# Hybrid decoder layer on one core: gating stage run as two passes over the tokens

## What is computed

```python
gate = jax.nn.sigmoid(_rmsnorm(h, g_ple) @ w_ple_gate)   # w_ple_gate 1024 x 1024
h = h + gate * (p @ w_ple)                               # w_ple 256 x 1024
...
y_prompt = _rmsnorm(hp, g_final)
y_sample = _rmsnorm(hs, g_final)
```

## Time and profile before

| what | value |
|---|---|
| median of 3 runs | 918.92 us (918.61 to 921.02) |
| profiled execution, its time | 919.41 us |
| its span | 917.6 us |
| granted TensorE clock, mean of full | 0.996 |
| TensorE busy | 904.3 us, 99% of the span |
| VectorE, ScalarE, GpSimd busy | 535.4, 370.0, 237.9 us |

### The profile page before, as it was taken

How to read it: one execution, slowest core, us unless ns; L and a number is a source line. 1 busy time by engine, 2 the same in 40 slices (tenths; PEclk the granted TensorE clock), 3 DMA queues, 4 the chain that set the end, 5 groups by cost and what they waited for, 6 DMA issues and landing times.

```text
span 917.6 us, 21039 instructions
## 1 busy us (share of the span) xinstructions
PE 904.3 (99%) x8016; PEld 894.6 (97%) x8016; DVE 535.4 (58%) x651; ACT 370.0 (40%) x511; POOL 237.9 (26%) x289
## 2 busy tenths in 40 slices
PE   9999999999999999999999999999999999999995
PEld 8999999999999999999999999999999999999995
DVE  6432279888765565665576666666666433435654
ACT  7323446556554555233343333333333222213433
POOL 0006078777111100004621111111111122213441
PEclk9999999999999999999999999999999999999998
DMA  7322534233245443533323333333333333332312
GB/s 227 104 87 88 184 94 105 59 98 97 72 129 157 114 131 108 192 119 100 92 70 95 90 91 91 91 91 91 91 91 109 96 94 94 94 92 66 107 36 94
DMA packets 176479, 94.84 MB, mean 103 GB/s; under 512 B 17888, under 2 KB 174960, under 8 KB 176016
## 3 DMA queue, kind: packets, MB, share of 16 engines
q1 hardware_dynamic: 149698, 80.61, 29.6%
q10 hardware_dynamic: 26736, 13.60, 5.5%
HBM read 86.25 MB, written 8.03 MB: 103 GB/s over the span
## 4 chain that ended last, share of the span: by engine, by line
PE 75%; DVE 5%; issue 3%; ACT 1%; ACTq 0%; DVEq 0%
PE acc L502 69%; DVE rs L1409 1%; DVE sfull L1396 1%; PE lvb L502 1%; DVE xs L1400 0%; PE mb L764 0%; PE lvb L728 0%; PE ob L743 0%; PE mb L747 0%; PE ob L742 0%; DVE ss L1449 0%; PE lvb L644 0%; DVE ot L1411 0%; DVE ss L1447 0%; PE lvb L852 0%
## 5 line engine op out<-in xcount | busy, mean ns | idle before, releaser
L908 ACT ACTIVATE whi<-raw 128x1024 fp32r<-128x1024 f32 (+2 forms) x132 | 146.8, 1112 | 369.6 <-PE acc L502 368.7
L1277 DVE TENSOR_TENSOR wlo<-raw,whi 128x1024 fp32r<-128x1024 f32 (+2 forms) x131 | 196.5, 1500 | 151.8 <-ACT whi L908 151.8
L502 PE MATMUL acc<-xah,whi 128*128 128x260 f32 x896 | 184.7, 287 | 0.0
L502 PE MATMUL acc<-xah,wlo 128*128 128x260 f32 x896 | 180.3, 283 | 0.0
L502 PE MATMUL acc<-xal,whi 128*128 128x260 f32 x896 | 179.9, 282 | 0.0
L502 PE MATMUL acc<-xbh,whi 128*128 128x260 f32 x816 | 165.0, 283 | 0.0
L502 PE MATMUL acc<-xbh,wlo 128*128 128x260 f32 x816 | 164.4, 283 | 0.0
L502 PE MATMUL acc<-xbl,whi 128*128 128x260 f32 x816 | 164.2, 283 | 0.0
L502 PEld LDWEIGHTS acc<-xah,whi 128*128 128x128 f32 x896 | 137.9, 188 | 1.5 <-issue 0.2
L502 PEld LDWEIGHTS acc<-xal,whi 128*128 128x128 f32 x896 | 138.0, 188 | 0.0
L502 PEld LDWEIGHTS acc<-xah,wlo 128*128 128x128 f32 x896 | 137.9, 188 | 0.0
(11 more groups left out here) (310 smaller groups left out, 1175.6 us busy)
## 6 DMA issues: line engine op xcount, KB each, us to landing
raw<-in_w_in SPq DMA_DIRECT2D x96, 256.0 KB, 3.1
raw<-in_w_up SPq DMA_DIRECT2D x88, 256.0 KB, 3.1
raw<-in_w_down SPq DMA_DIRECT2D x16, 384.0 KB, 3.5
raw<-in_w_down SPq DMA_DIRECT2D x16, 320.0 KB, 3.9
raw<-in_w_out SPq DMA_DIRECT2D x16, 256.0 KB, 3.1
raw<-in_w_ple_gate SPq DMA_DIRECT2D x8, 512.0 KB, 3.8
x_transposed<-xstg SPq DMA_DIRECT2D x1, 2080.0 KB, 7.6
hT<-x_transposed ACTq DMA_DIRECT2D x1, 2080.0 KB, 8.0
```

The lines of the kernel that those rows point to most:

```text
L502: mm = pe.matmul(sums[:, b, 0:HT], wt[slot][:, w], xx[:, c, b * HT:(b + 1) * HT], start=first and i == 0 and q == 0, stop=last and i == n ...
L908: act.activation(whi[k % 2][:, 0:n], raw[k % 2][:, 0:n], ACT.Copy).then_inc(hi_ready, 1)
L1277: dve.tensor_tensor(wlo[k % 2][:, 0:n], raw[k % 2][:, 0:n], whi[k % 2][:, 0:n].bitcast(fp), SUB).then_inc(lo_ready, 1)
```

## The change

The 520 tokens are taken in two passes (HSPLIT: 256 tokens, then 264). Step n of 16 makes channel tile n % 8 for the tokens of its pass: 24 gate and 6 embedding matmuls of 256 or 264 columns. The weights are loaded and copied to `whi` in both passes; the low parts of tiles 2 to 7 are kept in six new buffers `wlh`, and those of tiles 0 and 1 in `wlo`, so that VectorE subtracts in the first pass only. `tg`, `sgg`, `tp` and the PSUM sums are doubled. The addition to `hT` moves from VectorE to GpSimd for all steps but the last. PE's first two steps are interleaved (`first_steps`). The y transposes go by pairs of tiles and one pass's tokens (`y_pair`), the first behind step 3. The scale of the first 256 tokens is taken behind step 10, applied in step 12, and their two output DMAs are issued from there. VectorE's order at the end of G changes: the `xbl` of the last tile now comes ahead of the low part of unit H1.

```diff
-YSPLIT = 384
+YSPLIT = 448
+HSPLIT = (256, TT - 256)
...
-            for it in range(2):
-                for k in range(4):
-                    load("H", k, it, [wpg_v[:, :, it * 4 + k, :], wpl_v[:, :, it * 4 + k, :]])
-                if it == 0:
+            for n in range(2 * DC):
+                load("H", n, 0, [wpg_v[:, :, n % DC, :], wpl_v[:, :, n % DC, :]], low=n < DC + 2)
+                if n == 3:
...
+            def first_steps():
+
+                wait_high(0)
+                wait_low(0)
+                wait_parts(0, 0)
+                multiply(0, 0, range(7), end=False)
+                wait_parts(0, 1)
+                multiply(0, 1, range(2))
+                wait_high(1)
+                multiply(1, 0, range(7), (0, 1), end=False)
+                wait_low(1)
+                multiply(1, 0, range(7), (2,), end=False)
+                mean_square(1)
+                multiply(0, 0, (7,))
+                multiply(1, 1, range(2))
+                multiply(1, 0, (7,))
+
+            def gate_half(n):
+                wait_high(n)
+                if n == 2:
+                    pe.wait_ge(lv_free[0], L_Y // 2)
+                    multiply(n, 0, range(DC), (0, 1), end=False)
+                    wait_low(n)
+                    multiply(n, 0, range(DC), (2,))
+                else:
+                    wait_low(n)
+                    wait_parts(n, 0)
+                    multiply(n, 0, range(DC))
+                wait_parts(n, 1)
+                multiply(n, 1, range(2))
...
+            first_steps()
+            for n in range(2, 2 * DC):
+                gate_half(n)
+                if n == 3:
+                    y_pair(0)
+                elif n > 3 and n % DC and n % 2 == 0:
+                    y_pair(n // DC * 4 + n % DC // 2 - 1)
+                if n == DC:
+                    y_pair(3)
+                if n == DC + 2:
+                    pe.wait_ge(ssq_ready, 17 + DC)
+                    wait_misc(M_G, 0, 0, 0)
+                    token_sums(ssq, ((0, 0), (1, 128))).then_inc(misc_full, 1)
...
+            for n in range(2 * DC):
+                w = HSPLIT[n // DC]
+                if n == 0:
+
+                    half_done(0, 1)
+                    hi("H", 2, 0)
+
+                    act.activation(ssx[:, 6:7], eps[:], ACT.Sigmoid)
...
+                act.activation(sgg[n % 2][:, 0:w], tg[n % 2][:, 0:w], ACT.Sigmoid).then_inc(sig_ready, 1)
...
+                half_done(n, 1)
+                if 0 < n < 2 * DC - 2:
+                    hi("H", n + 2, 0)
+                act.wait_ge(h_new, n + 2)
+                act.activation(yT[:, n % DC, tokens(n)], hT[:, n % DC, tokens(n)], ACT.Copy,
+                               scale=vc[:, 32 + n % DC:33 + n % DC]).then_inc(y_ready, 1)
...
+                dve.tensor_tensor(tg[n % 2][:, 0:w], gate, rstd[:, tokens(n)], MUL).then_inc(acc_free[0], 1)
+                if n == 0:
+                    low(2)
+                half_done(n, 1)
+                dve.wait_ge(sig_ready, 12 + n + 1)
+                dve.wait_ge(h_new, max(n, 1))
+                dve.tensor_tensor(tp[n % 2][:, 0:w], acc[1][:, n % 2, 0:w], sgg[n % 2][:, 0:w],
+                                  MUL).then_inc(acc_free[1], 1)
...
+                if 0 < n < DC - 2:
+                    low(n + 2)
...
+            for n in range(2 * DC - 1):
+                j, w = n % DC, HSPLIT[n // DC]
+                pool.wait_ge(acc_free[1], SEC["H"][2] // 2 + n + 1)
+                if n == 0:
+                    step(pool.memset(ssq[:], 0.0))
+                taken()
+                pool.tensor_tensor(hT[:, j, tokens(n)], hT[:, j, tokens(n)], tp[n % 2][:, 0:w], ADD).then_inc(h_new, 1)
```

More of the change, by code:

```diff
@@ L345, in hybrid_layer @@
         ys_taken = sem("ys_taken")
+        y_half = sem("y_half")
         y_scaled = [sem(f"y_scaled{i}") for i in range(2)]
@@ L879, in token_sums @@
+            def token_sums(t, cols, first=True, last=True):
+                for i, at0 in cols:
                     n = 128 if i < 4 else NS
-                    mm = pe.matmul(mb[0:n, i:i + 1], t[:, i * 128:i * 128 + n], ones1024[:, 0:1],
-                                   start=not last and i == 0, stop=last and i == 3)
-                return mm
-            pe.wait_ge(ssq_ready, 24)
-            wait_misc(M_G, 0, 0, 0)
-            token_sums(ssq, False)
+                    mm = pe.matmul(mb[0:n, i:i + 1], t[:, at0:at0 + n], ones1024[:, 0:1],
+                                   start=first and i == cols[0][0], stop=last and i == cols[-1][0])
+                return mm
```

240 lines of the change are left out of this document (135 added, 105 removed).

## The result

The changed kernel takes **925.06 us** (median of 4 runs, 924.67 to 925.20) against 918.91 (918.61 to 921.02) for the kernel before in the same session: a ratio of 1.0059, 95% interval 1.0047 to 1.0071. It is slower by 6.15 us, more than the 0.3% that can be told from no change. The forecast was 923.5, range 919.5 to 926.2, slower with chance 0.66.

A forecast was written before the change was run, and what follows sets the result against it. PE bounds the kernel, busy 904.3 us, 99% of the span. Tail -3.7, PE work +0.9, waits +6.4 and clock +1.0 make +4.6 us; against 918.92 that is 923.5 us, range 919.5 to 926.2.

The forecast's parts named there:

- Tail: From PE's last product to the span's end: half-width chain and early output of two blocks give 3.7 us.
- rival 5: Output: the first two blocks leave only behind the last step, 2.6 us come back, 926.1 us; chance 0.02.
- PE: Work on PE in stage H: more transposes ahead of the last product (0.4) and four more sum records (0.45), together 0.9 us.
- First wait: PE waits 0.6 us for the low part of H1, GpSimd's sum going first; zero if VectorE goes first.
- Second: PE waits 1.15 us for the high part of H2, whose copy follows the roots on ScalarE.
- Third: PE waits 0.5 us for the low part of H2, behind the reciprocal and gate product on VectorE.
- Fourth: PE stands 4.1 us before step 3 for H3, whose copy is behind yT and second sigmoid on ScalarE.
- rival 2: Start-up chain shorter than laid out, clock holds: waits of 2.8 to 5.5 us, say 920.8 us; chance 0.25.
- Clock: PE's granted clock falls with the long stand: 1.0 us taken, bounds nothing and 3.6 us.
- Rival 3: Clock falls in the stand and stays down, step 3 wholly at half speed: 926.1 us; chance 0.10.
- From there on I find no further wait: After the fourth wait: no further PE waits; 0.3 us of load slack, which step 12's extra table loads fit.
- Rival 1: Start-up chain stays covered: 916.1 us, the change gains if waits total below 2.8 us; chance 0.08.

The follow-up runs named there:

- Experiment 4: Changed kernel with SP holding back the two early output DMAs until the first block of the last pass is scaled: 927.97 us.
- experiment 6: Changed kernel with GpSimd clearing ssq once the mean square is taken, rather than behind the first tp: 924.03 us.
- 12: Changed kernel with the order by tile alone, that is experiment 5 without the early clear of the sums and the early mean square: 922.33 us.
- experiments 3: Changed kernel with twelve unused matmuls of 128 columns on constants issued by PE ahead of step 3: 924.75 us.
- experiment 5: Changed kernel with the order by tile (first four steps take tiles 0 and 1 for both passes' tokens), early clear of sums and early mean square: 920.21 us.
- kernel 11: Experiment 5 with the copy of the first unit after the start-up moved ahead of the yT of step 1: 918.46 us.
- experiments 1: Changed kernel with the copy and low part of tile 3 moved ahead of step 0's yT and the second tp: 924.09 us.
- 8: Changed kernel with the addition to hT on VectorE again in every step: 923.31 us.
- 7: Changed kernel with the low part of H1 ahead of the last tile's xbl again, as before the change: 925.04 us.
- experiments 2: Changed kernel with the mean square and step 0's last chunk after the fourth instead of all seven chunks of step 1: 923.73 us.
- experiment 10: Experiment 5 with kernel 11's earlier copy, the addition to hT on VectorE, and the convolution-row stores issued six loads later: 919.83 us.

## Why the prediction was right, and where it was off

The direction, the mechanism and the range were right; the time was 1.6 us too low. Step by step:

- **Tail, 3.7 us forecast: 3.57.** The tail is E + 9.19 where E + 9.1 was forecast, the first DMA at E + 4.3 (4.2). Experiment 4 bears out that most of it is the output that leaves early, and so rival 5 falls.
- **PE, +0.9 us: 1.16.** Transposes and sums make 0.63 of it, less than forecast; the slow start of the products behind each stand and each group of transposes, 0.57, was not in the forecast.
- **First wait, 0.6: 0.66**, with GpSimd's sum first, then the low part, which took 2.60 us. **Second, 1.15: 0.83**, since PE itself needed 0.3 us more up to there than worked out (8.76 us from the first product, not 8.48), while the copy was ready when forecast. **Third, 0.5: 0.54.** **Fourth, 4.1: 3.96**, through each of the steps named: clear, addition, `yT`, second sigmoid, copy, low part. The waits make 5.99, forecast 6.4. Of rival 2 (chain shorter, 2.8 to 5.5 of waits) nothing came.
- **Clock, 1.0 us forecast: 1.35.** The fall came, and ended within step 3. Rival 3, that the clock stays down over all of step 3, did not come true in the profiled execution of this kernel. It all but did in that of experiment 4, which is the same program up to its output DMAs: there the term is 2.75 us. So this term was sized within its bounds, but 1.0 against 1.35 is partly luck. Its reason, that a stand of 0.79 us had not brought the clock down, is no measure for longer ones: the clock stayed full behind stands of 3.27 and 2.90 us and fell with one of 2.64. The Trainium skill, page "TensorE: Matmul & The Clock Gate", section "Loop structure matters more than you think", warns of matmuls run cold behind a long stand; by that rule the trace of this kernel agrees in kind, with 1.35 us as the price, and those of experiments 6 and 12 do not.
- **"From there on I find no further wait": this step failed.** It is worth 0.73 us, ahead of the second `yT` tile of a pair near the end. VectorE's two scalings of 1024 columns, which let the early output go, took 2.18 us beside GpSimd's sum and stand ahead of the gate product of step 13:

```profile
904.61 2.18 DVE L1795 TENSOR_SCALAR ytok<-ytok,rt 128x1024 f32<-128x1024 f32 x2
...
906.71 0.42 DVE L1769 TENSOR_TENSOR tg<-acc,rstd 128x264 f32<-128x264 f32 x1
```

  I had costed these two instructions in the tail that they leave, not in the step that they enter. The sentence that "the extra table loads in step 12 fit in that slack" fails with it. They hold the sigmoid of step 12 until 902.37, 1.8 us after its gate product (900.17 to 900.60), and the scalings stand behind that step on VectorE:

```profile
899.50 1.28 ACT L1312 ACT_TABLE_LOAD   x1
900.80 0.26 ACT L1312 ACTIVATE rt<-mb,eps 128x2 f32<-128x2 f32 x1
901.08 1.28 ACT L1317 ACT_TABLE_LOAD   x1
902.37 0.43 ACT L1317 ACTIVATE sgg<-tg 128x264 f32<-128x264 f32 x1
```

  PE was done with the gate sums of step 13 at 904.42, and their gate product began at 906.71. Either half of this delay, 1.8 us of table loads or 2.2 of scalings, is larger than the stand; no run takes them apart. In steps 4 to 13 PE didn't stand, as forecast. Part of the reason was not in the forecast: with the slow clock PE asked for its weights later. In experiments 3 and 6 the clock stayed full, a copy waited for its load, and a stand of 0.9 to 1.0 us came at step 5 or 6. The 0.3 us of slack that was named for the load was the right place and was not there: 3.8 us is the landing of the first DMA of a unit alone, and the whole unit takes 4.3.
- **The drain of a table load, left out: rightly.** After it the next instruction starts 0.01 us behind the load's end (852.22 and 1.28, then 853.51), as before. The Trainium skill, page "ScalarE: Activation LUTs", section "What ACT_TABLE_LOAD costs", adds a drain of about 1.38 us; no run here shows it.
- **Rival 1 (start-up covered)** came nearest to life in the order by tile, where waits of 2.0 us in experiment 5 and 0.8 in kernel 11 are left. Its point of decision, 2.8 us of waits, is too high: kernel 5 with 2.0 is 1.1 us above the kernel before in the median (not told apart), kernel 11 with 0.8 is 0.6 us below, so a straight line between them puts it near 1.2, an estimate. H to E is still 3.04 us over 61.82 in kernel 11: the stand of 0.81, 1.30 for transposes with small waits among them (4.33 against 3.03), 0.36 of sums, and 0.53 for the products' slower starts; the mean square is 0.03 longer.

The forecast missed 1.6 us, 6.15 against 4.6. The terms make 1.05 of it (0.73 for the step that I got wrong, 0.35 of clock, 0.13 of tail, 0.25 of work on PE beyond the forecast, less 0.41 in waits). The start of H, 0.35 earlier, takes as much off. The rest, 0.9, is how the profiled executions stand to their medians: that of before was 0.49 above its own, that of after 0.39 below.

## What to carry to other kernels

A stage that is split in halves keeps its total work on the bottleneck engine but halves the time in which the other engines must serve each weight unit; lay out the chain from the first normalisation to the second copied unit, engine by engine and in list order, before the split is made, since that is where reserve is lost. What helps is an order in which the buffers already filled serve twice as long, more than any single instruction moved earlier: each of those (experiments 1, 3, 6) moved part of the stand to a later step. The same edit can gain in one order and lose in another (the addition on VectorE, 1.75 us down and 1.2 up), as it depends on which engine the chain runs through just then. And before a difference of 1 us is put down to an edit, compare how long the slow clock lasted in both profiles: between the changed kernel and experiment 4 that alone made 1.4 us.

## What the runs showed of the hardware

- **The clock and the length of a stand don't go together one to one.** With stands of 3.27 us (experiment 6) and 2.90 (12) the granted clock stayed full; with 2.73 (8), 2.64 (1) and 3.96 (the changed kernel) it fell. In experiment 1 it fell 1.3 us after PE had started again. The slow time lasted 3.4 us in the changed kernel and in experiments 1, 7 and 8, and 6.8 in experiments 2 and 4, and experiment 4 is the changed kernel's program up to its output DMAs. Matmuls of 128 columns that do nothing useful kept it at the full level (3, one execution).
- **GpSimd and VectorE take whole turns, and the order is that of their starts.** Before, VectorE's low part starts beside GpSimd's square and ends 1.34 us after it (846.75), then GpSimd's sum, begun at 845.58, ends 1.17 us behind the low part. After, the sum starts first (845.23; 1.55 us, of which it spends some behind `xbl` that ends at 845.61), and the low part, begun at 845.53, ends at 848.13, 1.35 us behind it. So it goes on: the square of 256 columns, 0.61 us alone, is begun at 859.29 beside the low part of 858.77 and lasts 1.62, to 0.48 us behind its end. Each time the later one ends its own duration, less some 0.13 us, behind the earlier one. The Trainium skill, page "SBUF — State Buffer", section "🔬 SBUF: two separate sides", has it so, with a lock that the first to start holds for its whole instruction; by that rule the trace agrees. It is not so with every pair: `tp` of 857.67, which takes one input from PSUM, and GpSimd's sum of 857.67 ran side by side, each in its own time (0.42 and 0.73 us). The forecast, which let GpSimd's sum go first, gave 0.6 us for the wait that measured 0.66.
- **A fetch of instructions lies over the late loads.** A weight unit of 640 KB takes 4.3 us in the median from its first issue to its last landing. In each of the thirteen profiles with two passes one load issued between 858 and 865 took 5.0 to 6.2 us, and over each of these lies one packet of 16 KB on a DMA queue of the kind "instruction", which takes 1.3 to 2.4 us. In experiment 5 the view of the DMA queues from 858 to 864 us, in 40 slices, shows it as 2.1% of 16 engines' 6 us, that is 2.0 us:

```profile
GB/s 0 0 0 0 0 0 0 0 0 0 0 0 0 0 3 191 99 123 181 253 273 266 242 311 331 317 335 324 324 321 212 82 58 14 20 20 24 20 20 58
q8 instruction: 1, 0.02, 2.1%
```

  The bulk of that unit had come by 862.9, at up to 335 GB/s, then some 20 GB/s trickled on, and it landed only at 865.21. 20 GB/s is about a sixteenth of 335, as if one of 16 engines was still at work; that is an estimate from these two figures. Of the 164 weight loads of section H in all fourteen profiles 25 took over 5.1 us; such a packet came between issue and landing in 24 of them. The kernel before has such a packet too (858.93), but it came late in the load, which took 4.40 us. This is a coincidence in the traces, as no run moved the fetch; that the fetch is the cause is argued from it. The small stores ahead of the load are not the main cause (experiment 10).
